# Two RMS norms: root and reciprocal with tokens on partitions, spread by a product with a scaled identity

## What is computed

```python
def rms_norm(x, g):
    xf = x.astype(jnp.float32)
    var = jnp.mean(xf * xf, axis=-1, keepdims=True)
    return (xf * lax.rsqrt(var + EPS)).astype(x.dtype) * g

h_lat = rms_norm(x_lat, norm_g[i]) * (1.0 + sc_l[:, None]) + sh_l[:, None]   # ahead of the Fourier layer
h = h + token_mixer(rmsnorm(h, mix_norm[l]), ...)                            # ahead of the mixer
```

## Time and profile before

| | |
|---|---|
| median of three runs | 2444.23 us |
| profiled execution | 2442.99 us |
| its span | 2441.3 us |
| mean granted TensorE clock | 0.991 of 2.4 GHz |
| TensorE busy | 98% of the span |
| VectorE busy | 67% |
| ScalarE busy | 42% |
| GpSimd busy | 5% |

### The profile page before, as it was taken

The page is one execution under the profiler, slowest core; times in us unless marked ns, Lnnn a source line. Parts: engine busy times, 40 slices in busy tenths (PEclk is TensorE's granted clock), DMA queues, the critical chain, the costliest instruction groups (busy, mean ns, idle before and its releaser), DMA issues.

```text
span 2441.3 us, 46321 instructions
## 1 busy us (share of the span) xinstructions
PE 2382.5 (98%) x17214; PEld 2073.3 (85%) x17214; DVE 1641.4 (67%) x2395; ACT 1036.5 (42%) x1418; POOL 111.7 (5%) x138
## 2 busy tenths in 40 slices
PE   7999999999999989999999999989999999999997
PEld 3888888888888867888899999978999778888886
DVE  7578888888888855455564343469999975534446
ACT  4446545554654424333353222245545554322223
POOL 0012111111211100000000000000000000000000
PEclk9999999999999999999999999999999999999999
DMA  6212222222222322222222222223232222232223
GB/s 247 84 64 86 77 77 77 86 69 69 86 77 79 113 104 69 78 79 83 97 86 87 94 87 87 93 81 101 95 101 96 95 86 95 95 98 100 95 95 104
DMA packets 61990, 224.01 MB, mean 92 GB/s; under 512 B 6736, under 2 KB 8784, under 8 KB 61552
## 3 DMA queue, kind: packets, MB, share of 16 engines
q1 hardware_dynamic: 58992, 211.08, 25.8%
q0 software_dynamic: 2944, 12.19, 1.5%
HBM read 221.15 MB, written 2.10 MB: 91 GB/s over the span
## 4 chain that ended last, share of the span: by engine, by line
PE 60%; DVE 4%; ACT 1%; issue 1%; ACTq 0%; DVEq 0%
PE ps L511 59%; ACT w_hi L1128 1%; DVE w_lo L1690 0%; DVE n_tmp L1714 0%; DVE n_sq L1709 0%; DVE hb L2084 0%; DVE n_lo L1717 0%; DVE cv L2507 0%; DVE fin L2572 0%; DVE n_sq L2346 0%; DVE n_sum L1728 0%; DVE y_lo L1717 0%; DVE rt L1969 0%; DVE n_sq L2529 0%; PE ps L842 0%
## 5 line engine op out<-in xcount | busy, mean ns | idle before, releaser
L1128 ACT ACTIVATE w_hi<-w_raw 128x1024 fp32r<-128x1024 f32 (+1 forms) x360 | 377.9, 1050 | 911.5 <-PE ps L511 886.1
L1690 DVE TENSOR_TENSOR w_lo<-w_raw,w_hi 128x1024 fp32r<-128x1024 f32 (+1 forms) x360 | 435.5, 1210 | 215.0 <-ACT w_hi L1128 210.8
L511 PE MATMUL ps<-h_hi,w_hi 128*128 128x512 f32 x640 | 264.2, 413 | 4.3 <-DVE h_lo L1823 2.6
L511 PE MATMUL ps<-h_hi,w_lo 128*128 128x512 f32 x640 | 251.9, 394 | 0.0
L511 PE MATMUL ps<-h_lo,w_hi 128*128 128x512 f32 x640 | 251.6, 393 | 0.0
L511 PE MATMUL ps<-y_lo,w_hi 128*128 128x512 f32 x504 | 178.2, 395 | 7.4 <-DVE y_lo L1717 7.4
L511 PE MATMUL ps<-v_hi,w_hi 128*128 128x512 f32 x416 | 163.0, 392 | 3.4 <-DVE v_lo L2542 2.8
L511 PE MATMUL ps<-n_hi,w_hi 128*128 128x264 f32 (+1 forms) x576 | 155.2, 324 | 9.3 <-DVE n_lo L1717 8.5
L511 PE MATMUL ps<-v_hi,w_lo 128*128 128x512 f32 x416 | 161.9, 389 | 0.0
L511 PE MATMUL ps<-v_lo,w_hi 128*128 128x512 f32 x416 | 161.9, 389 | 0.0
L511 PE MATMUL ps<-n_hi,w_lo 128*128 128x264 f32 (+1 forms) x576 | 155.6, 325 | 0.0
(11 more groups left out here) (384 smaller groups left out, 5341.2 us busy)
## 6 DMA issues: line engine op xcount, KB each, us to landing
w_raw<-in_weights_dram SPq DMA_DIRECT2D x376, 512.0 KB, 3.2
ada_raw<-in_ada_weights_dram SPq DMA_DIRECT2D x4, 2048.0 KB, 20.7
gate_raw<-in_gate_weights_dram POOLq DMA_DIRECT2D x16, 512.0 KB, 3.6
x<-in_x_dram SPq DMA_DIRECT2D x1, 2048.0 KB, 12.4
x<-in_x_dram POOLq DMA_DIRECT2D x1, 2048.0 KB, 8.8
out_dram<-fin SPq DMA_DIRECT2D x16, 128.0 KB, 1.9
xc<-in_ctx_dram SPq DMA_DIRECT2D x1, 1024.0 KB, 19.0
masks<-in_masks_dram POOLq DMA_DIRECT2D x1, 512.0 KB, 5.0
```

Source lines behind the costliest of these rows:

```text
L511: last = nc.tensor.matmul(o, w, xp, start=start and n == 0, stop=stop and n == 2)
L1128: run(w_hi[:, s, 0:n], w_raw[:, s, 0:n], ACT.Copy).then_inc(hi_ready[s], 1)
L1690: tt(w_lo[:, s, 0:n], w_raw[:, s, 0:n], w_hi[:, s, 0:n].bitcast(F32), ALU.subtract).then_inc(lo_ready[s], 1)
```

## The change

In the two norms root and reciprocal are taken with tokens on partitions. The running sum and the last square are no longer added on VectorE. TensorE takes 128 tokens (or 88 of the 528) of the sum as the stationary operand and two columns of the matrix of 1/1024 as the moving one, into one PSUM bank per tile of tokens: four or six such products for the sum, while the last row is still being squared, and as many for the last square, accumulated on them. That gives the mean of each token on a partition, 128x4 (or 88x6) values in all. ScalarE takes the root and VectorE the reciprocal of these. VectorE multiplies an identity matrix, repeated for each tile, with these values and with 1024, and TensorE multiplies a matrix of 1/1024 with the result: that spreads the value of each token over all partitions, in PSUM, from where `norm_apply` reads it. Ahead of the Fourier layer ScalarE copies the spread values to SBUF at the end of the norm, for `fold`.

The last cut of a weight block in the residual loops (`after(3)` and `after(1)`) is moved from before the root to behind it on ScalarE, and from before the reciprocal to behind the scaled identity on VectorE. The fetch of the root's table is moved ahead of the last square, and the last trip of ScalarE's loop is written out for that.

```diff
+NORM_TILE = {T: P, TM: TM // 6}
+TOKEN_BANKS = (4, 5, 6, 7, 0, 1)
+            def norm_by_token(N, R, n, total, square, spread):
+                w = NORM_TILE[n]
+                at = [slice(t * w, (t + 1) * w) for t in range(n // w)]
+                pe.wait_ge(R["add"], KD + 1)
+                pe.wait_ge(R["res"], KD + 1)
+                for b_, c in zip(TOKEN_BANKS, at):
+                    nc.tensor.matmul(ps[0:w, b_, 0:2], total[:, c], ones_d[:, 0:2], start=True, stop=False)
+                pe.wait_ge(R["sq"], KD + 1)
+                for b_, c in zip(TOKEN_BANKS, at):
+                    last = nc.tensor.matmul(ps[0:w, b_, 0:2], square[:, c], ones_d[:, 0:2], start=False, stop=True)
+                last.then_inc(N["mean"], 1)
+                pe.wait_ge(N["turned"], 1)
+                for dst, diagonal in spread:
+                    last = nc.tensor.matmul(dst, ones_d[0:w], diagonal, start=True, stop=True)
+                last.then_inc(N["spread"], 1)
...
-            mean(N1, T, n1["sum"][:, 0])
+            norm_by_token(N1, RC, T, n1["sum"][:, 0], n1["sq"][:, 0], [(ps[:, 7], n1["tmp"][:, 1])])
...
-            mean(NMIX, TM, n2["sum"][:, 0])
+            norm_by_token(NMIX, RD1, TM, n2["sum"][:, 0], n2["sq"][:, 0],
+                          [(ps[:, 6 + q, 0:HALF], n2["tmp"][0:NORM_TILE[TM], 1, q * HALF:(q + 1) * HALF]) for q in range(2)])
...
+            def root_by_token(N, n):
+                w = NORM_TILE[n]
+                act.wait_ge(N["mean"], 1)
+                r_ = by_token[0:w].unsqueeze(2)
+                if n == TM:
+                    run(r_[:, 4:6], ps[0:w, 0:2, 0:1], ACT.Sqrt, bias=eps[0:w])
+                run(r_[:, 0:4], ps[0:w, 4:8, 0:1], ACT.Sqrt, bias=eps[0:w]).then_inc(N["root"], 1)
...
+                            if last and a and q == nb - 1:
+                                fetch_root()
                             if sums and square_first and q == nb - 1:
                                 square_one(R, m_, src(m_), sq, 2)
-                            after(a * nb + q)
+                            if not (last and a and q == nb - 1):
+                                after(a * nb + q)
...
-            fetch_root()
-            act.wait_ge(N1["sum"], 1)
-            root(N1, ps[:, 6], n1["sq"][:, 0])
+            root_by_token(N1, T)
+            after(3)
+            st.leave(1)
             norm_hi(N1, lambda k: nf_hi[:, k], lambda k: n1["tmp"][:, k % 2], lambda k: ada1[:, k, 0:1])
+            run(n1["sq"][:, 0], ps[:, 7], ACT.Copy).then_inc(N1["hi"], 1)
...
-                fetch_root()
-                act.wait_ge(N["sum"], 1)
-                root(N, ps[:, 6:8, 0:HALF], halves(n2["sq"][:, 0]))
+                root_by_token(N, TM)
+                after(1)
+                st.leave(1)
...
-            def norm_apply(N, src, gain, shift, tmp, rt_, hi, lo):
+            def turn_by_token(N, n, diagonal):
+                w = NORM_TILE[n]
+                r_ = by_token[0:w, 0:n // w]
                 dve.wait_ge(N["root"], 1)
-                own.link(v.reciprocal(rt_, rt_))
+                own.link(v.reciprocal(r_, r_))
+                stt(diagonal[0:w].rearrange("p (t c) -> p t c", c=w),
+                    ident[0:w, 0:w].unsqueeze(1).broadcast_to([w, n // w, w]), float(D),
+                    r_.unsqueeze(2).broadcast_to([w, n // w, w]), ALU.mult, ALU.mult).then_inc(N["turned"], 1)
+
+            def norm_apply(N, src, gain, shift, tmp, rt_, hi, lo, view=lambda t: t):
+                dve.wait_ge(N["spread"], 1)
...
-                        stt(tmp(k), src(k), gain(k), rt_, ALU.mult, ALU.mult).then_inc(N["tmp"], 1)
+                        stt(view(tmp(k)), view(src(k)), gain(k), rt_, ALU.mult, ALU.mult).then_inc(N["tmp"], 1)
...
-                        if last and a:
-                            close_sums(R, N, *sums)
-                        if cuts:
+                        if cuts and not (last and a):
                             after(a * nb + nb - 1)
...
+            turn_by_token(N1, T, n1["tmp"][:, 1])
+            after(3)
+            st.leave(1)
             own.link(stt(scale[:, 2], ada1[:, 8:16, 0:1].rearrange("p k n -> p (k n)"), 1.0,
                          vec[:, VEC["norm_g1"]:VEC["norm_g1"] + KD], ALU.add, ALU.mult))
...
+            dve.wait_ge(N1["hi"], KD + 1)
...
             def block_norm(N, name):
+                turn_by_token(N, TM, n2["tmp"][:, 1])
+                after(1)
+                st.leave(1)
```

More of the change, by code:

```diff
@@ L193, in program @@
         unused, warm = g.take("unused", [P, 1]), g.take("warm", [P, 1])
+        by_token = g.take("by_token", [P, 8])
         ada0 = g.take("ada0", [P, 16, 2])
@@ L342, in norm_sems @@
             return {k: sem(f"{tag}_{k}") for k in steps}
-        N0, N0C, N1, NMIX = [norm_sems(t, "sum", "mean", "root", "tmp", "hi", "lo") for t in ("n0", "n0c", "n1", "nmix")]
+        N0, N0C = [norm_sems(t, "sum", "mean", "root", "tmp", "hi", "lo") for t in ("n0", "n0c")]
+        N1, NMIX = [norm_sems(t, "mean", "root", "turned", "spread", "tmp", "hi", "lo") for t in ("n1", "nmix")]
         NFIN, NOUT = norm_sems("nfin", "mean", "root", "hi", "lo"), norm_sems("nout", "sum", "mean", "root", "lo")
-        NF1, NF2 = [norm_sems(t, "sum", "mean", "root", "hi", "lo") for t in ("nf1", "nf2")]
+        NF1, NF2 = [norm_sems(t, "mean", "root", "hi", "lo") for t in ("nf1", "nf2")]
         R0, R0C, RC, RF, RD1, RM, RD2 = [
@@ L1364, in _, with residual, one @@
             act_head(None, None, HEADS - 1)
-            def residual(R, trips, nb, src, sq, sums, ahead=True, done=0, square_first=True):
-                def one(i):
+            def residual(R, trips, nb, src, sq, sums, ahead=True, done=0, square_first=True, closing=False):
+                def one(i, last=False):
                     for a in range(2):
@@ L1371, in one @@
                         for q in range(nb):
+                            if last and a and q == nb - 1:
+                                fetch_root()
                             if sums and square_first and q == nb - 1:
                                 square_one(R, m_, src(m_), sq, 2)
-                            after(a * nb + q)
+                            if not (last and a and q == nb - 1):
+                                after(a * nb + q)
                         if sums and not square_first:
                             square_one(R, m_, src(m_), sq, 2)
-                if ahead:
+                if closing:
+                    with hinted(act, 0, trips - 1) as i:
+                        st.enter(i, 2 * nb)
+                        one(i)
+                    st.leave(trips - 1)
+                    st.enter(0, 2 * nb)
+                    one(trips - 1, True)
+                elif ahead:
                     with hinted(act, 0, trips) as i:
@@ L1394, in _ @@
                 square_one(RC, k, x1[:, k], n1["sq"][:, 0], 2)
-            residual(RC, (KD - EARLY) // 2, 2, lambda m_: row(x1, m_), n1["sq"][:, 0], True, done=EARLY)
-            fetch_root()
-            act.wait_ge(N1["sum"], 1)
-            root(N1, ps[:, 6], n1["sq"][:, 0])
+            residual(RC, (KD - EARLY) // 2, 2, lambda m_: row(x1, m_), n1["sq"][:, 0], True, done=EARLY, closing=True)
+            root_by_token(N1, T)
+            after(3)
+            st.leave(1)
             norm_hi(N1, lambda k: nf_hi[:, k], lambda k: n1["tmp"][:, k % 2], lambda k: ada1[:, k, 0:1])
+            run(n1["sq"][:, 0], ps[:, 7], ACT.Copy).then_inc(N1["hi"], 1)
             def gate_row(i, k):
@@ L1538, in feed_forward @@
                              lambda m_: row(hb, m_)[:, c0:TM], n2["sq"][:, 0, 0:n], final,
-                             not (final and last) or tag in half_done, square_first=tag not in half_done)
+                             not (final and last) or tag in half_done, square_first=tag not in half_done,
+                             closing=final and not last)
             def half_square(R, n, a, half):
@@ L1728, in add_square @@
                 tt(acc, acc, sq, ALU.add).then_inc(R["add"], 1)
[L1730 to L1733, removed]
             for s in range(2):
@@ L2107, in _ @@
             norm_apply(N1, lambda k: x1[:, k], lambda k: scale[:, 2, k:k + 1], lambda k: ada1[:, k, 0:1],
-                       lambda k: n1["tmp"][:, k % 2], n1["sq"][:, 0], lambda k: nf_hi[:, k], lambda k: nf_lo[:, k])
+                       lambda k: n1["tmp"][:, k % 2], ps[:, 7], lambda k: nf_hi[:, k], lambda k: nf_lo[:, k])
+            dve.wait_ge(N1["hi"], KD + 1)
             def fold(c, later=0):
@@ L2280, in block_norm @@
             def block_norm(N, name):
+                turn_by_token(N, TM, n2["tmp"][:, 1])
+                after(1)
+                st.leave(1)
                 norm_apply(N, lambda k: hb[:, k], lambda k: col(name, k), lambda k: zero[:],
-                           lambda k: n2["tmp"][:, k % 2], n2["sq"][:, 0], lambda k: n_hi[:, k, 0:TM],
-                           lambda k: n_lo[:, k, 0:TM])
```

(2 more changed lines are left out.)

2 lines of the change are left out of this document (1 added, 1 removed).

## The result

The changed kernel takes 2461.78 us (median of four runs, 2459.98 to 2462.60), the kernel before 2444.02 beside it (four runs, 2442.29 to 2445.59). The ratio is 1.0069, with a 95% interval of 1.0056 to 1.0081: slower by 17.8 us. The prediction was 2441.5, with a range to 2444.7 and a chance of 0.08 for slower. It was wrong.

What follows compares the result with a forecast made beforehand. TensorE, busy for 2382.5 of 2441.3 us, was taken as the bound, so only its pauses could give time. Gains of 1.6 + 1.1 = 2.7 us off 2444.2 gave 2441.5, range 2438.5 to 2444.7.

Steps and rivals of the forecast that it cites:

- part by part: First norm: lists removed and new pieces, each priced by its duration; first row's product at 910.86 instead of 912.45, gain 1.6 us.
- The sum for the first norm: Ahead of the Fourier layer: last square ends 906.23, first row's product follows at 910.86 with the spread at half clock.
- VectorE's cut and the two small instructions: First norm: moved weight cut, then scale and shift, end at 910.24, covered by the half-clock spread with 0.6 us left.
- The sum for the second norm: Ahead of the mixer: square ends 1611.85, first row 1617.33 instead of 1618.42; gain 1.1 us at half clock, 2.2 at full.
- Solved as in the prediction: Moment the clock fell, worked out from granted clock over a stretch; earlier falls 3.2, 4.1 and 2.0 us after dense work.
- rival 1: Both norms: TensorE still at full clock when the spreads run; gain 4.4 us, time 2439.8; chance 0.22, some with one spread only.
- choice of the half clock: Second norm: spread starts 4.7 us after dense work ended, later than any earlier fall, so it takes about 2.2 us.
- Rows read from PSUM: Both norms' row products on VectorE: reading the spread row from PSUM costs nothing; the skill's rule would cost 0.9 us.
- the two equal rows: VectorE's product of 512 columns takes 751 ns with one operand in PSUM and 751 with both in SBUF.
- Rival 2: Both norms: narrow products dearer, +1.1 and +1.5 us on the second halves; time 2443.7; chance 0.13.
- Rival 3: Both norms: PSUM operand makes VectorE's row products dearer, slower than before; at 0.62 us each +8.7, time 2450.2; chance 0.06.
- Rival 4: First norm: full clock returns only after the fifth row, losing the shift again, at worst 1.5 us; time 2443; chance 0.09.

## Why the prediction was wrong, point by point

**The step that failed** is the heading "part by part" itself: the change was taken as a list of instructions, each priced by its duration, and the sum had no term for the tile `by_token`. The line that takes it moves every activation by 32 bytes. Two runs give the term its size, 21.7 and 21.8 us, eight times the whole forecast gain. With it the sum would have been 2441.5 + 21.8 = 2463.3, with 2461.78 measured. None of the rows that the prediction read prices it. The trace of before has a hint in the mixer, where 512-column products read from 64 bytes behind a row's start and follow at a mean of 230.0 ns. And the step could have been seen as open without it: a tile taken ahead of all activations, in a kernel where TensorE is busy for 98%, where 1% of pace is 24 us.

**The sum for the first norm** held: 4.50 us measured, 4.63 forecast. Its narrow products took 1.05 as worked out from the earlier trace rows, the root 0.26 for 0.25, the reciprocal 0.18 for 0.20, the scaled identity 0.69 for 0.75, the spread 2.07 for 2.0, at half clock. VectorE's cut and the two small instructions ended 0.6 us before the spread did, as said. The whole shift went through: the row products began 3.26 us late instead of the 4.98 by which the square was late, and the piece behind the fifth row had the same length (5.27 for 5.25 in the earlier trace rows).

**The sum for the second norm** was too dear: 4.10 and 5.05 us in two kernels, against 5.48. The twelve narrow instructions took 1.08 and not 1.49, 0.08 apart, so a load of 88 columns does go faster, by just the 0.4 that stood as a bound. One wait was wrong the other way. The prediction let the twelve products of the running sum start when dense work ends and so be just hidden. They wait for VectorE's last residual row (`pe.wait_ge(R["res"], KD + 1)`): they start at 1617.97, 0.80 after dense work ended, and are still running when the square ends at 1618.59. The second twelve start at 1618.93, 0.34 behind the square and not 0.10. Ahead of the Fourier layer the like products were over before the square began, and the handoff was 0.05. The spread ran at full clock once (1.18) and at half once (2.13). The granted clock in the stretch from the end of the square to the scaled identity, and during the spread, in the changed kernel:

```profile
1618.60:1621.40 2.80, 1.41 (x19) 1.32 (x17) 0.88 (x2) 1.35 (x3) 0.00 (x0) 1.00 0.25 91
1621.40:1622.70 1.30, 1.18 (x4) 0.68 (x4) 1.25 (x3) 0.00 (x1) 0.00 (x0) 0.91 0.00 0
```

In the changed kernel without its tile, the same two stretches:

```profile
1611.10:1613.90 2.80, 1.41 (x18) 1.32 (x17) 0.88 (x2) 1.35 (x3) 0.00 (x0) 0.74 0.28 111
1613.90:1616.10 2.20, 2.13 (x4) 1.17 (x4) 1.24 (x2) 0.00 (x1) 0.00 (x0) 0.50 0.00 0
```

The seventh of the numbers is the granted clock, as a share of 2.4 GHz. The same instructions found 1.00 and then 0.91 in one kernel, 0.74 and then 0.50 in the other. Solved as in the prediction, the fall came at 1622.5 and at 1612.4, which is 5.3 and 2.8 us after dense work ended (1617.17 and 1609.67). The moment differs by 2.5 us between two executions of nearly one kernel, and that makes rival 1 true in this norm of the one and false in the other. The prediction's choice of the half clock was right in one of the two and so in part luck.

**Rows read from PSUM.** They cost nothing, as the two equal rows had it. In the groups of the changed kernel:

```profile
L1767 DVE SCALAR_TENSOR_TENSOR n_tmp<-x,scale,ps 128x512 f32<-128x512 f32 x8 | 5.9, 747 | 0.8 <-PE ps L572 0.6
```

747 ns now, 751 before. The larger fixed term for a PSUM source in the Trainium skill (VectorE: DVE Perf Modes, "The TRN2 errata"), 65 ns by an estimate from its figures, is not seen on this instruction.

**The rivals.** Rival 1 came true in full in one norm of one kernel and was worth the 0.95 us by which the spreads differ; in the kernel with the 256-column tiles moved it came in small part (1.80 and 1.91). Rival 2 did not come: 1.05 and 1.08. Rival 3 had the sign of the result and not its mechanism: VectorE's row products cost nothing more, and the loss is all in TensorE's products, in the layers ahead of the norms as behind them. Rival 4 did not decide. The clock did come back later in the first norm. TensorE started again at 918.15, and these are two stretches of the changed kernel:

```profile
921.00:922.00 1.00, 1.00 (x4) 0.78 (x3) 1.00 (x2) 0.29 (x1) 0.00 (x0) 0.50 0.00 0
...
923.00:924.00 1.00, 0.67 (x4) 0.23 (x3) 0.96 (x3) 0.72 (x1) 0.00 (x0) 1.00 0.00 0
```

With 0.63 in the microsecond between them, it rose at about 922.7, 4.6 us after the restart and not 3.2 as before, still ahead of the fifth row at 923.84.

**The whole without the tile**: 2440.12 measured, 2441.5 forecast. So the reasoning on the norm was sound within 1.4 us, which is inside the scatter of single runs (2437.48 to 2441.68), and the prediction of the change as it stands was not.

**What stays open.** Why TensorE's pace depends on the places of the two operands was not settled. That they meet in reading SBUF is an argument, not a result; shown is that no other engine is needed for it. Relations other than those named were not tried, and which ones are as good as none was not either: that the places must agree modulo 256 bytes fits all runs, but no run moved a group that had 227 ns by 128 or by 256. The small shortening of the 264-column products was not taken apart. Those of the first feed-forward block have rows of 528 x 4 bytes and halves of 264 x 4, which puts them at 0, 32, 64 and 96 past a multiple of 128 in turn whatever the tile's start is; that fits with a shift changing them by 0.9 ns only. Nearly half of these 0.9 is seen without any shift: the changed kernel without its tile has 122.6 ns where the kernel before has 123.0. The opposite sign at 256 columns is measured and not explained.

## What to carry to other kernels

When a change takes a new tile, however small, list what it moves, and see that the big operands keep their places relative to each other. Laid over a dead tile it cost nothing here; taking it last, behind all operands, was not tried, and 64 bytes instead of 32 was not enough. When TensorE is the bound, compare first the distance between the starts of products that the diff doesn't touch: one row of the chain (x1530, 347.08 and 357.11) told more than all rows of the changed stretch. And compare the clock time at the last point before the change: 5 us were lost there already.

## What the runs showed of the hardware

- Float32r products of 128x128 by 512 columns follow each other at 227 ns where moving operand and weights are as the kernel before has them (multiples of 256 bytes apart), at 234 with the moving operand 32 bytes further, at a mean of 230 with 64 and of 233.5 with the weights 32 further; with both 32 further at 227 again. In this kernel with 6085 such products the first step cost 21.7 and 21.8 us.
- A multiple of 128 bytes is not enough: 576 products whose operands lay at multiples of 128 behind the weights, every other one a multiple of 256, followed at a mean of 232.2 ns.
- Products of 256 columns go the other way: 120 ns at the same place, 117 with the moving operand 32 or 64 bytes further, 119 with the weights 32 further.
- An operand off its place slows neighbouring products too (medians of 232 ns where only every third product's moving operand was moved; one run).
- The slower pace needs no other engine: 232.8 against 226.9 ns in stretches where VectorE, ScalarE, GpSimd and the DMAs did nothing.
- The granted clock fell 2.8 and 5.3 us after dense work at the same place of two nearly equal kernels, with the same narrow products in between.
- A product of 512 float32 columns put into a pause did not keep the clock at full for the product behind it, in the one trace of it: the clock fell under the idle product itself, which took 1.35 and 1.78 us instead of 1.02.
